# Sparse attention on one core: values stationary, scaled transposed probabilities of four heads moving in three rounded passes

## What is computed

```
p_c = masked_softmax(s_c, dist_c >= 0)
o_cmp = jnp.einsum('bghtj,bjge->bghte', p_c, v_cmp)
...
p = masked_softmax(s, (dist >= 0)[:, :, None])
return jnp.einsum('bghqk,bgqke->bghqe', p, vg)
...
o = gates[..., 0:1] * o_cmp + gates[..., 1:2] * o_slc + gates[..., 2:3] * o_win
return o.astype(u.dtype) @ w_out
```

## Time and profile before

| | us |
|---|---|
| median of 3 runs | 2742.45 (2741.99 to 2743.88) |
| the profiled execution | 2741.93 |
| its span | 2740.1 |
| PE busy | 2714.2 (99%) |
| PE weight load busy | 2261.2 (83%) |
| DVE busy | 1684.5 (61%) |
| ACT busy | 1344.0 (49%) |
| stage 2's attention steps | about 1430 to 1680 of the span |

### The profile page before, as it was taken

The page is one execution under the profiler, slowest core; times in us unless marked ns, Lnnn a source line. Parts: engine busy times, 40 slices in busy tenths (PEclk is TensorE's granted clock), DMA queues, the critical chain, the costliest instruction groups (busy, mean ns, idle before and its releaser), DMA issues.

```text
span 2740.1 us, 32409 instructions
## 1 busy us (share of the span) xinstructions
PE 2714.2 (99%) x13136; PEld 2261.2 (83%) x13136; DVE 1684.5 (61%) x2280; ACT 1344.0 (49%) x1952; POOL 62.3 (2%) x85
## 2 busy tenths in 40 slices
PE   9999999999999999999999999999999999999998
PEld 7788888888888888888888888888888888887877
DVE  5666665565666666545645555666666664466666
ACT  6645444554444444434544555644444443355565
POOL 0000000000000000000100000000000000000002
PEclk9999999999999999999999999999999999999999
DMA  7764655756666666666665434666666666665444
GB/s 231 135 139 123 116 125 124 205 192 200 193 193 192 193 197 194 192 193 196 205 194 154 123 108 162 195 196 186 199 193 194 194 194 193 193 206 164 161 138 132
DMA packets 213494, 480.61 MB, mean 175 GB/s; under 512 B 15584, under 2 KB 16480, under 8 KB 212704
## 3 DMA queue, kind: packets, MB, share of 16 engines
q1 hardware_dynamic: 210848, 467.32, 59.1%
q0 software_dynamic: 2352, 11.17, 1.2%
q10 hardware_dynamic: 144, 0.05, 0.0%
HBM read 476.38 MB, written 2.10 MB: 175 GB/s over the span
## 4 chain that ended last, share of the span: by engine, by line
PE 90%; DVE 5%; ACT 2%; issue 1%; DMA 1%; POOL 0%; SPq 0%; ACTq 0%; POOLq 0%
PE PS L1116 19%; PE PS L1118 19%; PE PS L1117 19%; PE PS L1163 8%; PE PS L1164 8%; PE PS L1165 8%; DVE WL L2183 1%; DVE WORK L2350 1%; ACT WH L1657 1%; PE PS L1379 1%; PE PS L1263 1%; PE PS L1515 1%; PE PS L1282 1%; PE PS L1091 1%; DVE XL L2183 0%
## 5 line engine op out<-in xcount | busy, mean ns | idle before, releaser
L2183 DVE TENSOR_TENSOR WL<-RAW,WH 128x1024 fp32r<-128x1024 f32 x826 | 1010.5, 1225 | 817.1 <-ACT WH L1657 814.7
L1657 ACT ACTIVATE WH<-RAW 128x1024 fp32r<-128x1024 f32 x830 | 875.3, 1056 | 924.8 <-PE PS L1118 610.7
L1116 PE MATMUL PS<-WH,UTH 128*128 128x512 f32 x2396 | 951.9, 397 | 3.3 <-DVE WL L2183 1.8
L1118 PE MATMUL PS<-WH,UTL 128*128 128x512 f32 x2396 | 934.3, 390 | 0.0
L1117 PE MATMUL PS<-WL,UTH 128*128 128x512 f32 x2396 | 933.7, 390 | 0.0
L1116 PEld LDWEIGHTS PS<-WH,UTH 128*128 128x128 f32 x2396 | 450.4, 188 | 99.3 <-issue 5.2
L1118 PEld LDWEIGHTS PS<-WH,UTL 128*128 128x128 f32 x2396 | 449.9, 188 | 96.1
L1117 PEld LDWEIGHTS PS<-WL,UTH 128*128 128x128 f32 x2396 | 450.7, 188 | 88.3
L1163 PE MATMUL PS<-WH,HTH 128*128 128x512 f32 x656 | 255.2, 389 | 0.0
L1164 PE MATMUL PS<-WL,HTH 128*128 128x512 f32 x656 | 255.2, 389 | 0.0
L1165 PE MATMUL PS<-WH,HTL 128*128 128x512 f32 x656 | 255.2, 389 | 0.0
(11 more groups left out here) (420 smaller groups left out, 2211.7 us busy)
## 6 DMA issues: line engine op xcount, KB each, us to landing
RAW<-in_ffn_w_gu SPq DMA_DIRECT2D x352, 512.0 KB, 4.4
RAW<-in_ffn_w_down SPq DMA_DIRECT2D x176, 512.0 KB, 4.6
RAW<-in_ab_w_in SPq DMA_DIRECT2D x128, 512.0 KB, 4.8
RAW<-in_nsa_w_in SPq DMA_DIRECT2D x80, 512.0 KB, 3.6
RAW<-in_w_in SPq DMA_DIRECT2D x64, 512.0 KB, 4.1
RAW<-in_ab_w_out SPq DMA_DIRECT2D x32, 512.0 KB, 4.2
RAW<-in_nsa_w_out SPq DMA_DIRECT2D x32, 512.0 KB, 4.3
RAW<-in_w_out SPq DMA_DIRECT2D x16, 512.0 KB, 4.4
```

The costliest lines, as they stand in the source:

```text
L1116: e.matmul(o, lh, wh[:, j], start=k + j == 0, stop=False)
L1118: x = e.matmul(o, ll, wh[:, j], start=False, stop=k + j == NKT - 1)
L1657: e.activation(wh, raw, ACTF.Copy).then_inc(*a_hi.inc(s))
L2183: e.tensor_tensor(wl, raw, wh.bitcast(F32), ALU.subtract).then_inc(*v_lo.inc(s))
```

## The change

**Values.** `n` for the values (columns 3584 and 4608 of the input product) writes them rounded (VH, ACT) and DVE adds a new 128x512 operation for the rest (VL), two for each column block. The compressed values get the same (VC: rows 0 to 14 and 64 to 78 the rounded ones, 32 to 46 the rest).

**Probabilities.** `sx` has a third DVE operation: P is multiplied by r in place (128x60, 128x512 or 128x1024). `pt` on PE waits for that instead of for ACT. `pt` on ACT rounds (T, and T0 for branch 0, written twice), and `pt` has a new part on DVE: the rest, PSUM minus the rounded copy, 128x512 for each tile of keys, written into the buffer of P (T0 rows 64 to 78 for branch 0).

**Product.** `pv` has the values stationary (128x128) and T moving, all four heads at once: 512 columns, in three fp32r passes, high by high, low by high, high by low, for each tile of keys. Branch 0 has no `pv` of its own: its 79 rows, which stand for all three products, open the sum of branch 1 in the same bank. `pv` on ACT copies branch 1's bank out, DVE adds branch 2's bank to it; scaling is gone from both.

**Output.** O now has channels on partitions, so `ot` has no PE part: ACT and DVE read O in SBUF, with the axes put in order.

```diff
-                    yield from need(("pt", g - 2, i, br))
+                    yield from need(("pv", g - 2, i, br) if br else ("pt", g - 2, i, 0))
...
-            put("pv", g, i, br)
+            if br:
+                put("pv", g, i, br)
...
             def ot(st, k):
+                if st == 2:
+                    return
...
             def pt(g, i, br):
...
-                on.wait_ge(*(v_ns.of("mc", g, i) if br == 0 else a_ns.of("ex", g, i, br, 3)))
+                on.wait_ge(*v_ns.of("p", g, i, br))
...
             def pv(g, i, br):
-                T = NT[g % 2][i]
                 b = take("pv", g, i, br)
...
-                    for kk in range(kn):
-                        x = e.matmul(o, T[:, 4 * kk + h], ZN[:, kk, c:c + 128], start=kk == 0, stop=kk == kn - 1)
+                c = (3584, 4608)[br - 1]
+                hi, lo = NT[g % 2][i], nsa_lo(g, i, br)
+                if br == 1:
+                    on.wait_ge(*v_ns.of("vc"))
+                    on.wait_ge(*v_ns.of("tl", g, i, 0, 0))
+                    e.matmul(b, VC[0:79, g], T0[i][0:79], start=True, stop=False)
+                on.wait_ge(*v_ns.of("vl", c, 1))
+                on.wait_ge(*v_ns.of("tl", g, i, br, i))
+                for kk in range(i + 1):
+                    vh, vl = VH[c][:, kk, 128 * g:128 * g + 128], VL[c][:, kk, 128 * g:128 * g + 128]
+                    e.matmul(b, vh, hi[:, kk], start=br == 2 and kk == 0, stop=False)
+                    e.matmul(b, vl, hi[:, kk], start=False, stop=False)
+                    x = e.matmul(b, vh, lo[:, kk], start=False, stop=kk == i)
...
             def pt(g, i, br):
+                if br == 0:
...
+                    for r in (0, 32):
+                        e.activation(T0[i][r:r + 15], banks.ap("pt", g, i, 0, 0)[0:15], ACTF.Copy).then_inc(*a_ns.inc("pt", g, i, 0, r))
+                    return
...
+            def pv(g, i, br):
+                if br == 1:
+                    on.wait_ge(*p_ns.of("pv", g, i, 1))
+                    e.activation(ZN[:, i, 512 * g:512 * g + 512], banks.ap("pv", g, i, 1),
+                                 ACTF.Copy).then_inc(*banks.empty(a_ns, "pv", g, i, 1))
...
+            def n(a, t):
+                if a in VH:
...
+                    e.scalar_tensor_tensor(out=VL[a][:, t], in0=banks.ap("acc", 2, c, t), scalar=HR[:, t:t + 1],
+                                           in1=VH[a][:, t].bitcast(F32), op0=ALU.mult,
+                                           op1=ALU.subtract).then_inc(*banks.empty(v_ns, "acc", 2, c, t))
...
+                p = nsa_p(g, i, br)
+                e.tensor_tensor(p, p, bc(rs, p.shape[2]), ALU.mult).then_inc(*v_ns.inc("p", g, i, br))
...
+            def pt(g, i, br):
...
+                on.wait_ge(*p_ns.of("pt", g, i, br, i))
+                for kk in range(i + 1):
+                    on.wait_ge(*a_ns.of("pt", g, i, br, kk))
+                    e.tensor_tensor(nsa_lo(g, i, br)[:, kk], banks.ap("pt", g, i, br, kk), NT[g % 2][i][:, kk].bitcast(F32),
+                                    ALU.subtract).then_inc(*banks.empty(v_ns, "pt", g, i, br, kk))
...
-                for h in range(4):
-                    up = banks.empty(v_ns, "pv", g, i, br) if h == 3 else v_ns.inc("pv", g, i, br, h)
-                    e.scalar_tensor_tensor(out=O[:, h], in0=b[:, h], scalar=rs[:, h:h + 1], in1=O[:, h],
-                                           op0=ALU.mult, op1=ALU.add).then_inc(*up)
+                if br == 2:
+                    O = ZN[:, i, 512 * g:512 * g + 512]
+                    on.wait_ge(*p_ns.of("pv", g, i, 2))
+                    on.wait_ge(*a_ns.of("pv", g, i, 1))
+                    e.tensor_tensor(O, banks.ap("pv", g, i, 2), O, ALU.add).then_inc(*banks.empty(v_ns, "pv", g, i, 2))
```

More of the change, by code:

```diff
@@ L812, in build @@
         ident = MK[:, 896:1024]
+        BIGR, WORKR = over("BIGR", 2 * CHUNKS_EVEN, big_at), over("WORKR", 10752, work_at)
+        T0 = [sb(f"T0{i}", 512, F32R)[:] for i in range(2)]
         BLANK = BIG[:, 0:128]
@@ L896, in build @@
         KC = WORK[:, 1472:1532].rearrange("p (j g) -> p j g", g=4)
-        VC = w3(1536, 512, 4)
+        VC = v3(WORKR[:, 1536:2048], 4)
+        VH = {c: v3(BIGR[:, 0:2 * 5168], 2)[:, :, c:c + 512] for c in (3584, 4608)}
+        VL = {3584: v3(WORKR[:, 6144:7168], 2), 4608: v3(BIGR[:, 0:2 * 5168], 2)[:, :, 4096:4608]}
         GT = v3(SM[:, 32:128], 2)
@@ L1750, in n @@
                     e.activation(ZN[:, t, a:b], S2[:, t], ACTF.Copy, scale=HR[:, t:t + 1]).then_inc(*a_z.inc("n", a, t))
+                elif a in VH:
+                    on.wait_ge(*p_mm.of(col_end[2, c]))
+                    on.wait_ge(*g_rs.of("r", "pre", 2))
+                    e.activation(VH[a][:, t], banks.ap("acc", 2, c, t), ACTF.Copy,
+                                 scale=HR[:, t:t + 1]).then_inc(*a_z.inc("n", a, t))
                 else:
@@ L2012, in cm_o @@
                 else:
-                    e.activation(VC[0:15], v3(b[0:15, :], 4), ACTF.Copy).then_inc(*banks.empty(a_ns, "cm_o", part))
+                    on.wait_ge(*g_ns.of("vc0"))
+                    for r in (0, 64):
+                        e.activation(VC[r:r + 15], v3(b[0:15, :], 4), ACTF.Copy).then_inc(*a_ns.inc("vc", r))
             @step
@@ L2058, in pt @@
                     on.wait_ge(*p_ns.of("cm_h", 1))
-                for kk in range(1 if br == 0 else i + 1):
+                for kk in range(i + 1):
                     on.wait_ge(*p_ns.of("pt", g, i, br, kk))
-                    e.activation(T[0:n, 4 * kk:4 * kk + 4], v3(banks.ap("pt", g, i, br, kk)[0:n, :], 4),
-                                 ACTF.Copy).then_inc(*banks.empty(a_ns, "pt", g, i, br, kk))
+                    e.activation(T[:, kk], banks.ap("pt", g, i, br, kk), ACTF.Copy).then_inc(*a_ns.inc("pt", g, i, br, kk))
+            @step
+            def pv(g, i, br):
[3 more added lines that the diff above has]
+                                 ACTF.Copy).then_inc(*banks.empty(a_ns, "pv", g, i, 1))
             @step
@@ L2234, in ot @@
                 on.wait_ge(*a_ut.of("ot", st, k))
[L2235 to L2241, removed]
+                if st == 2:
+                    e.tensor_tensor(by_token(UTL, k), by_group(k), by_token(UTH, k).bitcast(F32),
+                                    ALU.subtract).then_inc(*v_ut.inc("ot", st, k))
+                    return
+                e.scalar_tensor_tensor(out=UTL[:, k:k + 2], in0=v3(banks.ap("ot", st, k), 2), scalar=GN[:, k // 8:k // 8 + 1],
+                                       in1=UTH[:, k:k + 2].bitcast(F32), op0=ALU.mult,
+                                       op1=ALU.subtract).then_inc(*banks.empty(v_ut, "ot", st, k))
             @step
@@ L2528, in gt, with cm_o @@
             @step
+            def n(a, t):
+                if a in VH:
+                    c = [x[0] for x in NSA].index(a)
+                    on.wait_ge(*a_z.of("n", a, t))
+                    if a == 4608:
+                        on.wait_ge(*p_ns.of("kt", 3, 1))
+                    e.scalar_tensor_tensor(out=VL[a][:, t], in0=banks.ap("acc", 2, c, t), scalar=HR[:, t:t + 1],
+                                           in1=VH[a][:, t].bitcast(F32), op0=ALU.mult,
+                                           op1=ALU.subtract).then_inc(*banks.empty(v_ns, "acc", 2, c, t))
+                    v_ns.also("vl", a, t)
+            @step
+            def cm_o(part):
+                if part:
+                    on.wait_ge(*a_ns.of("vc", 64))
+                    e.tensor_tensor(VC[32:47], v3(banks.ap("cm_o", 1)[0:15], 4), VC[0:15].bitcast(F32),
+                                    ALU.subtract).then_inc(*banks.empty(v_ns, "cm_o", 1))
+                    v_ns.also("vc")
+            @step
             def gt():
@@ L2900, in gpsimd @@
             e.memset(one_b, 1.0).then_inc(*g_nm.inc("one"))
+            for i in range(2):
+                e.memset(T0[i].bitcast(F32), 0.0).then_inc(*g_ns.inc("t0", i))
             on.wait_ge(*g_nm.of("mhalf"))
```

83 lines of the change are left out of this document (45 added, 38 removed).

## The result

| | before | changed |
|---|---|---|
| median | 2743.15 us (4 runs, 2741.99 to 2743.88) | 2757.55 us (4 runs, 2756.94 to 2761.85) |
| ratio, 95% interval | | 1.0056 [1.0041, 1.0071] |
| the profiled execution | 2741.93 us | 2761.85 us |
| its span | 2740.1 us | 2760.1 us |

The profiled execution of the changed kernel is the longest of its four, 4.3 us over the median, so I don't read the cost of the change from its span. It leaves out what differs from run to run ahead of the attention (slot 463 started between 1.3 us earlier and 2.8 us later than before in thirteen profiled runs).

A forecast was written before the change was run, and what follows sets the result against it. The prediction took PE as busy 99% but the attention's in-order DVE and ACT loop as what new work would delay: 30.9 us of added waits less 18.6 off PE gave +12.3, taken as +13, so 2755.5 us, range 2738 to 2769.

The forecast's parts named there:

- the walk through the loop: Attention's DVE and ACT chain, followed step by step: new DVE work delays weight rests and pv, adding 30.9 us of PE waits.
- What PE loses: PE's own work in pv and ot falls by 16.6 us; with two bank waits gone, 18.6 us off PE.
- rival D: 79-row matmul or float32 to fp32r turns cost over 0.23 us; at 0.4, 4 us more; within own case's 0.62.
- What DVE gets: DVE gets 47.6 us of new work and loses 23.5, net 24 us in 250.
- Group 2: Two VL of 4608 stand ahead of sx in slot 499; PE waits 6.8 and 3.1 us.
- Group 0: Weight rest of slot 468 comes 2.3 us late, and pv (0, 0, 1) 2.5 us.
- The waits behind the long ones: Second PE waits: 2.9 us at pv (1, 1, 1) in group 1, 3.1 us in group 2.
- The clock: PE's clock in the attention, 1.00 in every window read; what follows longer waits was priced at nothing.
- rival C: PE's clock falls after waits of 5 and 6.8 us, costing 2 to 5 us each: 2760 to 2775; chance 0.10.
- Wrong if PEclk drops below 1.00: Sign against the forecast: a window in 1430 to 1700 with PEclk under 1.00 would mean rival C.
- Rival A: New DVE work fits into the slack, so only PE's saving of 16.6 to 18.6 us counts: 2725; chance 0.18.
- Rival B: No change: waits come at half size, 15 us, giving 2739, up to 2748 with two thirds; chance 0.10.

The follow-up runs named there:

- e8: Changed kernel with 64 useless 512-column matmuls ahead of five pv, where PE stands longest, to keep PE busy: 2759.11 us, 1.0062.
- e5: Changed kernel with every instruction kept, DVE's order in each slot now score, row maximum, then rest, 1/sum and P by r: 2739.51 us, 0.9986.
- e6: Changed kernel with the row maximum first in DVE's order and P by r of branches 1 and 2 on POOL: 2737.64 us, 0.9980.
- e1: Changed kernel with every pv one slot later in the order, nothing else: 2763.54 us, 1.0075.
- e4: Changed kernel with its rests but without DVE's product of P by r: 2743.11 us, 0.9999.
- e11: Kernel before with P by r added on DVE and sx placed behind the row maximum in each slot: 2742.26 us, 0.9999.
- e9: Kernel before with only the order changed, sx behind the scores and the row maximum in each slot: 2739.76 us, 0.9991.

## Why the prediction came out right

It said 2755.5 us and +13; measured were 2757.55 and +14.4, and +17.1 in the repeated run. The direction and the mechanism, the walk through the loop, were right. That the sum came within 2 to 4 us was also luck: from slot 463 to 520 the forecast had 7.1 us too many of new waits and no slow matmuls, of which there were 9.7 us, and it took 2.7 us too many off PE. By its steps:

- **What PE loses.** 16.6 us were foretold; by the table above it is 13.9. The matmul of 79 rows starts the next one 0.24 us later, like the others, and `ot` is gone. But the 80 matmuls of the new `pv` take 20.5 us at full clock, not 18.2: the first one behind a float32 step starts the next 0.31 to 0.33 us later (1620.98 to 1621.30). So rival D, which put such turns at 0.4 us and the sum at 4 us, is true in about half its size. PE's stretches without waits win ground as they should (4.5 us between slots 501 and 508).
- **What DVE gets.** +24 us foretold, +23.6 measured; 1.22, 0.69 and 0.68 us a piece.
- **The walk through the loop.** This step carried the result. Slot 492's WL was to end 1.4 us later than before and slot 493's 2.6, and PE to wait 5.0 us. Counted from slot 491's WL it is 1.6 and 3.1 us, and the wait is 5.25 us. Group 2: 6.8 foretold, 6.51 measured. Slot 481: 0.8 and 0.66. Group 0: 2.3 and 2.40 at the weights, but 2.5 and 0.69 at `pv`. Group 3's last wait: 3.1 and 3.20.
- **What was over-counted.** The waits behind the long ones: 2.9 and 3.1 us foretold in groups 1 and 2, 0.36 and 1.34 measured. Together with group 0 that is most of the 7.1 us by which the waits fell short (23.8 us of the 24.9 are new, where 30.9 stood; the two on ACT stand in the kernel before too).
- **What was priced at nothing.** The clock. The sum took it as 1.00, and it fell: 0.50 in the 4 us behind the long wait of group 1, as rival C had it. The Trainium skill (TensorE: Matmul & The Clock Gate, section on the HAM clock gate) says that PE's clock falls to half after idleness, and the trace agrees. The price of rival C, 2 to 5 us a group, did not come on top: in groups 1 and 2 the two errors are in part one. The slow matmuls took up time in which the second waits would have stood, and those waits came back in e8, with the clock kept up (2.33 and 2.93 us, near the 2.9 and 3.1 foretold). "Wrong if PEclk drops below 1.00" was thus the wrong test for C. The test should have been whether a wait is still behind the slow stretch.
- **Rival A** assumed slack in the loop. Its own condition, "the loop shorter by 5 us for each group", is nearly what e5 makes (17.35 us for three passes, not 21.81), and there it comes out in part: 2739.5 and, in e6, 2737.6, not 2725. 10 and 11 us of waits on the rest and on P by r are left in these two.
- **Rival B** had the new waits at half their size; they came at 23.8 of 30.9 us. Its upper end is wrong by its own sum: two thirds of 30.9 less 18.6 is +2, so 2744.5 and not 2748.

The clock in 4-us windows around the first long wait (columns as above):

```profile
1548.00:1552.00 4.00, 2.80 (x13) 1.98 (x11) 3.62 (x5) 1.47 (x8) 0.00 (x0) 1.00 0.43 131
1552.00:1556.00 4.00, 0.00 (x0) 0.00 (x0) 2.78 (x6) 2.75 (x6) 0.00 (x0) 0.67 0.14 16
1556.00:1560.00 4.00, 3.95 (x16) 3.56 (x16) 1.12 (x1) 2.84 (x9) 0.00 (x0) 0.50 0.32 115
1560.00:1564.00 4.00, 3.64 (x17) 2.67 (x15) 3.72 (x6) 3.44 (x7) 0.00 (x0) 0.97 0.34 90
```

Where I was wrong is in the experiments. I expected e1 to cure what the walk had found at one place, and did not walk the banks. I expected P by r alone to cost the kernel before 3 to 8 us, and it cost 19, because I priced the delay of the loop and neither what it does to the banks that the old scaling on DVE holds nor the clock (7.8 us of slow matmuls). The gains of e4, e5 and e11 were all larger than I expected.

What stays open: how much of the place's cost goes through the row maximum and how much through the banks; what the slow matmuls cost outside group 1; and whether the old or the new form of `pv` is the better one when the order is right, since e5 and e9 can't be told apart and P by r on POOL has no counterpart in the old form.

## What to carry to other kernels

When two in-order engines hand work to each other in a loop, the order inside the loop can be worth more than the amount of work: put first what the other engine waits for, and the independent operations behind it. Here the same instructions cost 20 us more ahead of the row maximum than behind it, with DVE busy 62% of the span in either case. Work taken off the engine that looks like the bound (13.9 us here) gives nothing if it comes with work inside such a loop (the kernel became 14 to 17 us slower); and before a waiting consumer is moved later, walk the buffers that it holds and needs.

## What the hardware showed that I had not expected

- After PE had stood 5.25 us its granted clock was 0.50, the 1.2 GHz level, and 512-column matmuls started 0.43 us apart instead of 0.23. After a wait of 2.4 us they did too (1461.35, 1461.77, 1462.20, the window 1460 to 1464 having 0.65). Further on in the same slot's matmuls the distance was 0.23 again (1464.72, 1464.95; 1560.37, 1560.60).
- The halved clock cost nothing in group 1, where another wait stood behind it (e8), and 1 to 3 us in group 3, where none did.
- A product of 128x1024 numbers with a factor for each head takes POOL 2.13 to 2.20 us (one of eight took 2.81) and one of 128x512 1.04, beside a DVE that is busy 28 of 40 us.
